# Weight units between column sums, a new VectorE order, zeroed products and two later weight loads in a two-layer trunk step

## The reference

```python
mod = silu(cond) @ ada_w[l] + ada_b[l]          # 9 rows of 1024: shift, scale, gate of three sub-layers
h = rmsnorm(x, norm_pre) * (1 + scale) + shift
y = swiglu(h, gate, up, down)                   # or the token mixer
x = x + 0.5 * gate_row * rmsnorm(y, norm_post)  # 1.0 for the mixer
```

## Time and profile before

| | |
|---|---|
| median of 3 runs | 2199.2 us (2198.91 to 2199.8) |
| the profiled execution, its own time | 2199.55 us |
| its span, first to last instruction | 2197.8 us |
| PE busy | 2142.3 us (97%) |
| DVE, ACT, POOL busy | 892.9, 930.4, 1233.3 us |
| mean granted clock of PE | 0.983 |
| HBM traffic | 305.35 MB read, 141 GB/s over the span |

### The profile page before, as it was taken

How to read it: one execution, slowest core, us unless ns; L and a number is a source line. 1 busy time by engine, 2 the same in 40 slices (tenths; PEclk the granted TensorE clock), 3 DMA queues, 4 the chain that set the end, 5 groups by cost and what they waited for, 6 DMA issues and landing times.

```text
span 2197.8 us, 33516 instructions
## 1 busy us (share of the span) xinstructions
PE 2142.3 (97%) x13737; PEld 2048.6 (93%) x13737; DVE 892.9 (41%) x1572; ACT 930.4 (42%) x1389; POOL 1233.3 (56%) x972
## 2 busy tenths in 40 slices
PE   7999999999899999999999999999998999999998
PEld 7999998988899999999989999899888999899998
DVE  4221126446766454222251221445576564621111
ACT  4222333345766543223333233324567646423232
POOL 2766553434478454666646666453444965376663
PEclk9999999999999999999999999999999999899998
DMA  8555674433223374445554437553232245244432
GB/s 291 179 155 181 231 247 145 127 86 90 68 87 105 115 280 125 132 138 175 182 180 134 144 120 239 185 154 92 79 88 77 87 125 174 67 143 126 127 118 72
DMA packets 313073, 311.46 MB, mean 142 GB/s; under 512 B 9924, under 2 KB 293848, under 8 KB 312920
## 3 DMA queue, kind: packets, MB, share of 16 engines
q1 hardware_dynamic: 305815, 303.55, 44.4%
q10 hardware_dynamic: 7104, 5.77, 0.8%
HBM read 305.35 MB, written 3.93 MB: 141 GB/s over the span
## 4 chain that ended last, share of the span: by engine, by line
PE 78%; DVE 8%; ACT 6%; POOL 4%; issue 2%; SPq 1%; DMA 1%; DVEq 0%; ACTq 0%
PE X L603 55%; PE S L603 9%; PE Ab L603 5%; POOL w_lo L543 2%; PE S L639 1%; PE Ab L639 1%; PE X L732 1%; ACT w_hi L1097 1%; POOL dec L571 1%; POOL dec L570 1%; PE X L840 1%; PE S L869 1%; ACT p L1296 1%; PE X L922 1%; SPq L521 1%
## 5 line engine op out<-in xcount | busy, mean ns | idle before, releaser
L543 POOL TENSOR_TENSOR w_lo<-raw,w_hi 128x512 fp32r<-128x512 f32 (+1 forms) x872 | 1156.0, 1349 | 931.1 <-ACT w_hi L1097 922.1
L1097 ACT ACTIVATE w_hi<-raw 128x1024 fp32r<-128x1024 f32 (+1 forms) x436 | 453.3, 1042 | 652.8 <-PE X L603 621.0
L603 PE MATMUL X<-h_hi,w_hi 128*128 128x384 f32 x1600 | 537.9, 336 | 4.4 <-DVE h_lo L1662 3.5
L603 PE MATMUL X<-h_lo,w_hi 128*128 128x384 f32 x1600 | 535.6, 335 | 0.0
L603 PE MATMUL X<-h_hi,w_lo 128*128 128x384 f32 x1600 | 535.5, 335 | 0.0
L603 PEld LDWEIGHTS X<-h_hi,w_hi 128*128 128x128 f32 x1600 | 301.2, 188 | 11.9 <-issue 5.9
L603 PEld LDWEIGHTS X<-h_lo,w_hi 128*128 128x128 f32 x1600 | 301.2, 188 | 0.0
L603 PEld LDWEIGHTS X<-h_hi,w_lo 128*128 128x128 f32 x1600 | 301.2, 188 | 0.0
L1730 DVE TENSOR_TENSOR prod<-X,silu 128x768 f32<-128x768 f32 x44 | 42.1, 958 | 549.7 <-PE X L603 549.7
L603 PE MATMUL X<-act_hi,w_hi 128*128 128x384 f32 x704 | 235.7, 335 | 0.0
L603 PE MATMUL X<-act_hi,w_lo 128*128 128x384 f32 x704 | 235.2, 334 | 0.0
(11 more groups left out here) (404 smaller groups left out, 3135.7 us busy)
## 6 DMA issues: line engine op xcount, KB each, us to landing
raw<-in_w_in SPq DMA_DIRECT2D x124, 512.0 KB, 3.8
raw<-in_ffn_gate SPq DMA_DIRECT2D x88, 512.0 KB, 3.8
raw<-in_ffn_up SPq DMA_DIRECT2D x88, 512.0 KB, 3.8
raw<-in_ffn_down SPq DMA_DIRECT2D x80, 512.0 KB, 3.5
raw<-in_ada_w SPq DMA_DIRECT2D x48, 512.0 KB, 3.6
hold<-in_ada_w SPq DMA_DIRECT2D x29, 512.0 KB, 6.4
first_w<-in_ada_w SPq DMA_DIRECT2D x16, 512.0 KB, 8.8
hold_a<-in_ada_w SPq DMA_DIRECT2D x16, 512.0 KB, 8.3
```

Source lines behind the costliest of these rows:

```text
L543: ins = nc.gpsimd.tensor_tensor(slot(w_lo, u)[:, part], raw_of(u)[:, part], slot(w_hi, u)[:, part], SUB)
L603: mm = nc.tensor.matmul(dst, w[:, k, m * 128:m * 128 + 128], r_, start=start and k + j == 0, stop=stop and k == u.nk - 1 and j == 2)
L1097: A(slot(w_hi, u), raw_of(u), ACT.Copy).then_inc(hi_ready[u.split], 1)
```

## The change

Four things are changed.

1. `gap` puts one unit behind each column sum, and moves four units from behind the second `spread` to ahead of it; units 17 to 22 are no longer done before the head but behind its tiles 1, 2 and 3, two each. The head is now worked off with both accumulators for every k.
2. `joint` adds tiles 0 and 1 to x ahead of the wait for `cross_ready`, so that tile 2 is the only one behind it. In the loop, `low(0)` and `low(1)` follow the norm of tile 1, and the tile added to x is k+2, behind `low(k-1)`.
3. PE multiplies zeros (two tiles that VectorE clears first): ten products of 384 columns before anything else, and five behind the transposes of the vectors.
4. SP issues the third and fourth weight unit behind the twelfth `first_w` unit and not behind the eighth.

```diff
             for n, u in enumerate(PHASES["first"]):
-                if n in (4, 8):
-                    stream(n // 2 - 2, n // 2)
+                if n in (4, 12):
+                    stream(n // 4 - 1, n // 4 + 1)
...
-                for k in range(4):
+                for k in range(KT):
                     pe.wait_ge(S["h_ready"], seen.next("h_ready"))
-                    part(head[0], k)
-                    part(head[1], k)
-                for k in range(4, KT):
-                    pe.wait_ge(S["h_ready"], seen.next("h_ready"))
-                    part(head[2], k)
-                for k in range(4, KT):
-                    part(head[3], k)
+                    part(head[k // 4 * 2], k)
+                    part(head[k // 4 * 2 + 1], k)
+                    if k:
+                        for u in riders[2 * k - 2:2 * k]:
+                            ada_unit(u)
...
+            def busy(n):
+                for _ in range(n):
+                    nc.tensor.matmul(X[1][:, 1, 0:T], h_lo[:, 0, 0:128], h_hi[:, 0, :], start=True, stop=True)
+
+            pe.wait_ge(S["zeros_ready"], 1)
+            busy(10)
             pe.wait_ge(S["const_in"], 16)
...
+            busy(5)
...
                 add_to_x(0)
+                add_to_x(1)
...
-                step(V.tensor_tensor(y[:, 1, :], y[:, 1, :], SPREAD[0], MUL))
+                step(V.tensor_tensor(y[:, 2, :], y[:, 2, :], SPREAD[0], MUL))
                 inverse_root()
-                step(V.tensor_tensor(x[:, 1, :], x[:, 1, :], y[:, 1, :], ADD))
-                add_to_x(2)
+                step(V.tensor_tensor(x[:, 2, :], x[:, 2, :], y[:, 2, :], ADD))
...
+                    dve.wait_ge(S["norm_ready"], seen.next("my_norm"))
                     if k == 1:
-                        ada_take(units[7])
-                    if k:
+                        low(0)
+                        low(1)
+                        ada_take(units[KT - 1])
+                    if k > 2:
                         low(k - 1)
-                    if k + 3 < KT:
-                        add_to_x(k + 3)
-                    dve.wait_ge(S["norm_ready"], seen.next("my_norm"))
+                    if k and k + 2 < KT:
+                        add_to_x(k + 2)
```

More of the change, by code:

```diff
@@ L255, in build @@
         g_free = [sem(f"g{b}_free") for b in range(4)]
-        names = ("const_in table_in mask_in rows_in lam_in_s lam_ready x_in xs_in rows_turned vec_ready c_ready c_zero x_turned x_copied x_ready "
+        names = ("const_in table_in mask_in rows_in lam_in_s lam_ready x_in xs_in rows_turned vec_ready c_ready c_zero zeros_ready x_turned x_copied x_ready "
                  "x_sq_ready y_sq_ready g_made c_made y_added c_added first_copied parts_ready x_sum_made cross_ready mg_factor_made spread_ready r_ready sum_ready root_ready norm_ready hh_ready h_ready silu_ready act_ready "
@@ L691, in stream, with by_tiles @@
                     mm.then_inc(unit_done[u.split], 1)
-            def by_tiles(head):
+            def by_tiles(head, riders=()):
                 def part(u, k):
@@ L740, in spread, with y_sums @@
                 mm.then_inc(S["spread_ready"], 1)
-            def y_sums():
+            def y_sums(between=()):
                 pe.wait_ge(S["y_sq_ready"], seen.next("y_sq_ready", KT))
@@ L746, in y_sums @@
                 token_sums(S5, prod[:, 0, :], True, False)
+                for u in between:
+                    ada_unit(u)
                 pe.wait_ge(S["parts_ready"], seen.next("parts_ready"))
@@ L753, in gap @@
                     ada_unit(u)
-                y_sums()
+                y_sums(units[2:3])
+                ada_unit(units[3])
                 pe.wait_ge(x_free[0], seen.value(("xf", 0)) + 1)
                 token_sums(X[0][:, 0, 0:NB], y_sum, True, False)
-                ada_unit(units[2])
+                ada_unit(units[4])
                 pe.wait_ge(S["r_ready"], seen.next("r_ready"))
@@ L761, in gap @@
                 token_sums(X[0][:, 1, 0:NB], silu[:, 1, :], True, False)
+                ada_unit(units[5])
                 pe.wait_ge(S["parts_ready"], seen.next("parts_ready"))
                 token_sums(X[0][:, 0, 0:NB], part, False, True)
+                ada_unit(units[6])
                 pe.wait_ge(S["c_made"], seen.next("c_made", KT))
                 token_sums(X[0][:, 1, 0:NB], prod[:, 1, :], False, True).then_inc(S["cross_ready"], 1)
-                for u in units[3:7]:
+                for u in units[7:11]:
                     ada_unit(u)
@@ L770, in gap @@
                 spread(SPREAD[1], r_t)
-                for u in units[7:]:
+                for u in units[11:2 * KT]:
                     ada_unit(u)
-                return by_tiles
+                return lambda head: by_tiles(head, units[2 * KT:])
             def x_sums():
@@ L2087, in _ @@
                 dve.sem_inc(name, 1)
+            V.memset(h_lo[:, 0, :].bitcast(f32), 0.0)
+            V.memset(h_hi[:, 0, :].bitcast(f32), 0.0).then_inc(S["zeros_ready"], 1)
             V.memset(eps[:, :], EPS)
```

## The result

The median of 14 runs of the changed kernel is 2212.5 us (2202.5 to 2218.0), that of 14 runs of the kernel before beside them 2199.1 (2196.6 to 2203.7): ratio 1.0056, 95% interval 1.0047 to 1.0066. The forecast was 2189.3 with a range up to 2209; size and sign are both wrong. The profiled execution took 2209.95 us, its span is 2208.2 against 2197.8: 10.4 us to explain. It is one of the faster executions of the 14, so the median lost 3 us more than is taken apart here.

A forecast was written before the change was run, and what follows sets the result against it. Bound by half-clock PE work in the gaps, VectorE setting the first gap's end, PE the next three. Five gaps -18.6 and opening +2.7 give -15.9; with one fall -10.3, from 2199.55 to 2189.3 us, range 2182 to 2209.

The forecast's parts named there:

- What bounds the kernel: In all five gaps TensorE's clock drops below 1.00; VectorE sets the first gap's end, PE the second to fourth.
- What a fall costs: In a gap of the new order, a fallen clock costs about 5.6 us against one that holds.
- The price of a fallen gap against the kernel before: Fallen clock: +2.3 us in the first gap, +1.7 in each of the next three, +0.7 in the last.
- All gaps hold: Clock stays up in all five gaps: -18.6 us there, -15.9 with the opening.
- no sum follows another without a unit: In the gaps, the argument against the rival that two or three fall, which was put at 2197.7 us.
- the clock falls in nearly all gaps: Rival: five falls give +10.8 us, 2210, slower; chance 0.20 for four or five falls.
- The gain of a held gap: Held clock: -3.3 us in the first gap, -3.9 in each of the next three, -3.6 in the last.
- the same instructions in another order: VectorE's norm loop in each gap: only reordered, so its last `h_lo` also comes 3.3 us earlier.
- The additions ahead of `cross_ready`: VectorE's adding two tiles to x in the gap ends at 337.5, before 338.2, and costs nothing; 0.7 us slack.
- The opening: Before the first gap: later weight loads delay tiles 2, 4 and 6; +2.7 us, bounds +0.4 to +5.
- ACT's two times: In the opening, the fourth weight unit's `w_hi` at 36.0-36.1 us, `h_hi` of tile 2 at 37.1.
- The zeroed products: 0: In the opening, ten run while PE has nothing, five cost 0 to +0.2 us; taken as 0.

The follow-up runs named there:

- gaps_only: The changed kernel with its opening (load order, zeroed products) put back as before, gaps as changed: 2208.8 us, ratio 1.0043.
- gaps_dense: gaps_only plus two dense products, results unread, beside each of the five units between the sums: 2199.3 us, ratio 1.0001.
- dve_only: The kernel before with only VectorE's new order (`joint`), PE's order and opening as before: 2202.8 us, ratio 1.0015.
- dense_late: gaps_dense with VectorE's wait for each norm moved behind the low half and addition that follow: 2197.4 us, ratio 0.9990.
- pe_dense: gaps_dense with VectorE's old order: 2212.0 us, ratio 1.0057.
- opening_only: The changed kernel with the gaps put back as before, keeping the later weight loads and zeroed products: 2200.1 us, ratio 1.0001.
- opening_act: opening_only with ACT doing the high halves of tiles 2 and 3 ahead of those of the third and fourth weight unit: 2201.2 us, ratio 1.0005.
- zeros_only: The kernel before plus the fifteen zeroed products alone, loads in the old order: 2200.0 us, ratio 1.0003.
- gaps_late: gaps_only with VectorE's wait for each norm moved behind the low half and addition that follow, no dense products: 2210.2 us, ratio 1.0048.
- dense_mix_late: dense_late with two dense products beside each of the first two units and one beside each of the other three: 2193.5 us, ratio 0.9982.
- dense_front: dense_late with two dense products beside each of the first two units and none beside the other three: 2192.4 us, ratio 0.9976.
- zeros_ten: The kernel before plus only the first ten zeroed products, loads in the old order: 2197.4 us in a single run.
- loads_only: The kernel before plus the later loads of the third and fourth weight unit, no zeroed products: 2200.0 us, ratio 1.0004.

## Why the prediction was wrong

- **What bounds the kernel, and what holding is worth: right. What a fall costs: too small in two gaps.** In gap 4 the clock held and the second spread came at 11.2 us instead of 14.0. A fall in the new order was to cost 5.6 us; in the change and `gaps_only`, the same gap fell in one and held in the other three times: gap 3 is 42.2 and 36.0 long, gap 4 41.3 and 36.2, gap 5 38.6 and 35.5, so a fall cost 6.2, 5.0 and 3.1. The price of a fallen gap against the kernel before was forecast as +2.3 in gap 1, which came at +1.7, and +1.7 in gaps 2 and 3, which came at +3.8; the clock was low for 13.7 us there, where before it is 10.2.
- **The step that failed: "All gaps hold", with "no sum follows another without a unit" as the reason.** Four of five fell, with a clock of 0.62 to 0.71 over the gap and the second spread 14.1 to 17.2 us in, where the gap that held has 11.2. I had two rows on either side (two units did not hold it, sums behind dense small units did) and took a unit in each pair as enough. `gaps_dense` and `gaps_only` differ by the dense products alone, and by 9.5 us: that the clock makes the loss is shown. Why it falls in one gap and not in the next stays open. The rival "the clock falls in nearly all gaps", at 2210 with a chance of 0.20, is what happened; that its number comes so near is partly luck, since it was added up from five falls at +8.1 in all, and the profile has four that cost +9.2 and one gap that gained 2.1.
- **The gain of a held gap: right in sign, too big.** -3.9 was forecast, -2.1 and -2.3 measured in gaps that PE set before; -3.6 in the last, -3.2 measured. Two terms: the norm is 2.8 us earlier, not 3.3 (a sum with its unit takes 1.33 us, not 0.745 + 0.43 = 1.18), and VectorE's loop is 1.0 us longer. I had called it "the same instructions in another order"; `dve_only` shows that the order costs it, `dense_late` that the wait right behind each norm is 0.55 of it. The rest wasn't taken apart.
- **The additions ahead of `cross_ready`: right.** VectorE had 0.29 us left there (0.7 forecast) in the held gap. `pe_dense` shows what they are for: with the old order the norm is 1.1 us late.
- **The opening: +2.7 forecast, between -1.5 and +2.2 measured.** ACT's two times were right, and with the loads alone tiles 2 and 4 came within 0.4 us of their forecast. "The zeroed products: 0" missed PE's stop ahead of tile 0, which the old opening does not have; tile 4 came at 48.8 to 51.8 in the four profiles with all fifteen of them, and the last dense product ahead of gap 1 starts at 333.9 in their mean, 2.2 us behind the mean with the old opening. The old opening also differs from one execution to the next, from 45.0 to 49.8 (47.4 in the mean over 14 profiles), and the one that I reckoned from was the fastest. And in the three executions that had the stop and the old gaps (`opening_only`, `opening_act`, `zeros_only`), gaps 1 and 2 were 2.7 and 1.5 us shorter than in the one before, so that little was left of the delay. What ties the two together stays open; in these gaps the clock fell later (5.3 to 5.7 us in, not 3.4) and was low for 6.8 us, not 10.2.
- **Busy and the clock.** In gap 2 of the changed kernel PE is busy for 18.05 of 18.40 us at a mean clock of 0.63. By the Trainium skill, "TensorE: Matmul & The Clock Gate", Part 1, TensorE's being busy has its clock released; the measurement differs from that, now in the new order too, and the measurement decides.

## What to carry to other kernels

Mixing small products with other small ones held the clock in 3 of 20 gaps here: read the granted clock beside the busy share, and try a few dense products whose result nobody reads soon behind the last dense work. Seven of them in each gap turned a kernel that loses 0.5% (`gaps_late`) into one that gains 0.2% (`dense_mix_late`); four of them, `dense_front`, gain 0.24%. When two engines' orders belong together, change both: PE's alone lost 0.64% and VectorE's alone 0.15%, and both together lost less than PE's alone. And take the length of a stretch from more than one execution before costing an edit of 2 us.

## What was not expected of the hardware

- **The clock falls at a different place each time.** Gap 2, with the same instructions in it, was 36.8 us long in one execution and 38.3 in another (`opening_only` and before, which differ in the opening), by where in the gap the clock fell. The changed kernel's 14 runs lie 15.5 us apart, those of the kernel before 7.1, and the spread goes with the mean granted clock: 0.984 to 0.986 in the three fastest runs of the change (2202.5 to 2205.1 us), 0.977 or 0.978 in the four slowest (2215.7 to 2218.0).
- **PE stops at a fixed place in its own instructions.** The trace has a packet of 16 KB on the instruction queue close to the start of each stop in the opening, from 1.3 us ahead of it to 0.9 us behind, and PE goes on 2.5 to 2.8 us after it: packet at 35.32 and next product at 37.81 (before), 29.98 and 32.77 (after), 31.42 and 34.01 (`zeros_only`), 28.76 and 31.36 (`zeros_ten`), 35.98 and 38.45 (`loads_only`). The place moves with the number of instructions ahead. That PE waits for its own instructions is the reading that fits both. The packets at 28.56 and 41.80 in the kernel before have no such stop behind them. That the load queues' traffic makes the fetch slow is possible (347 to 352 GB/s around these stops, in both kernels) but was not tried.
